# Order of the input products and the latent queries' path in the first block of a two-part network on Trainium2

## Chip, cores and metric

The kernel runs on one core of one Trainium2 chip. The metric is the device time of one execution in microseconds; of the kernel before, three runs gave a median of 1709.43 us (1709.2 to 1711.75).

## What is computed

Two networks of depth 2 follow each other on 256 latent tokens (width 1024). The first also carries 256 context tokens. The change is in the first, whose block is, cut to what matters:

```
def first_block(...):
    for i in range(DEPTH):                      # 2
        hc = modulate(rms_norm(x_ctx, g_norm1[i]), csh1, csc1)
        h = modulate(rms_norm(x_lat, g_norm1[i]), sh1, sc1)
        # h @ w_in -> q (6 heads x 64), k, v (2 x 64), cq (256), ckv (128), k_rope (32), pool input (256)
        # qm = rms_norm(cq) @ w_uq : 6 latent queries x 96;  km, vm = rms_norm(ckv) @ w_ukv
        # q, k normed per head and rotated; of qm and km the last 32 columns are rotated
        mix = concat([attention(q, k, v), attention(qm, km, vm),
                      multiscale_pool(pool_in, w_pool, ls_pool)]) @ w_out
        x_lat = x_lat + gt1 * mix
        x_lat = x_lat + gt2 * sq_relu_mlp(modulate(rms_norm(x_lat, g_norm2[i]), sh2, sc2))
        # block 0 does the same for the context tokens; block 1 only takes keys and values from them
```

Context tokens attend to context keys alone, latent tokens to both. The second network (two layers with differential attention and an mLSTM) isn't touched.

## The kernel before

Every engine has its own program, written out by hand, and they meet in semaphores; no scheduler moves anything. Weights come from memory through a ring of three slots of 2048 KB that SP fills (L991); a slot's transfer starts when the slot three before it has been used. Large products are made of three fp32r products: ScalarE rounds a granule of a weight (two chunks of 128 rows) to its high part (`hi_to`, L1892), VectorE makes the low part (`lo_to`, L2509), and TensorE's `in_granule(n, m)` (L1444 to L1446) multiplies granule m of input slot n for up to four tiles of 128 tokens: high by high, high by low and low by high. The granules of a block's input slots are w0 to w0+11, four in each slot.

Below, PE is TensorE, ACT is ScalarE, DVE is VectorE and POOL is GpSimd. `w_in` has three input slots in a block. Slot A holds keys, values, the latent keys' source and the shared rope key (416 columns); slot C the latent queries' source cq and the pool's input (512; 256 in block 1, where p0 and p1 are multiplied apart, L1412, from weights that `shift_products`, L2569 and L2572 on DVE, scales); slot B the attention's queries (384). The order is A, C, B. Block 0 multiplies four token tiles, block 1 for C and B two.

Between and behind these products lies what this text calls the units: transposes (`turned_over`, L1456), latent keys and values (L1472), latent queries qm (L1489), and on the way to each the norms and rotations. ACT takes products out of PSUM (L2011, L2028, L2034, L2042, L2046; Tk, Tkm, Tqm, Tq are the transposed keys, latent keys, latent queries and queries) and takes roots (L1953 to L1955). DVE sums squares (L2580), refines the roots (L2586, L2587), multiplies by cosines (L2655, L2666, L2673) and scales (L2648, L2682). POOL makes the halves swapped and multiplied by sines (L1067), adds them (L1079, L1107, L1115), scales the rope keys (L1094) and makes the pool's window sums (L1137 to L1156). The last things before the attention are 24 (block 1: 12) transposes Tqm and 12 (6) transposes Tq.

The attention runs in steps j, one 128-row tile of queries for a pair of heads in each. Block 0 has 24 steps (two sets of tokens), block 1 has 12. In step j PE makes the scores of j (L1568), transposes the weights of j-2 (L1586) and every second step multiplies by the values (L1600); DVE takes the maximum (L2746) and scales by the reciprocal sum (L2756, L2757), ACT takes the exponential (L2103) and copies transposed weights (L2093). The pairs of latent heads begin at step 12 in block 0 and at step 6 in block 1. In block 0 some steps also hold products for the modulation (`mod_products`, L1320; `mod_column`, L1330; their sums on DVE L2450 and L2451).

At the start, `shift_hi` (ACT, L1912) and `modulated_norm` (DVE, L2549 and L2521) make the eight chunks of the normed, modulated tokens as a high and a low part, while ACT and DVE split the first weights between them:

```
if not which and k in (1, 4, 6):
    lo_to(first_gran["win", i] + {1: 1, 4: 2, 6: 3}[k])
```

## Time and profile before

| | us |
|---|---|
| median of three runs (lowest, highest) | 1709.43 (1709.2, 1711.75) |
| the profiled execution's own time | 1707.64 |
| its span in the trace | 1705.9 |
| PE busy | 1638.3 (96%) |
| DVE, ACT, POOL busy | 1149.5, 907.6, 487.8 |
| attention of block 0, of block 1 begins at | 134.62, 702.95 |

The span is what lies between the first and last instruction of the profiled execution, 1.7 us short of that execution's time. In the page, busy time is a share of the span; "PEclk" is the granted clock of PE as a share of full speed, its mean 0.988 here. A row of the timeline has start and duration in us, engine, line, operation, what it writes and reads, the count of merged instructions, and in brackets the idle time before it and what ended that.

### The profile page before, as it was taken

What the parts mean: (1) busy time and instruction counts of PE and PEld (TensorE: products, weight loads), DVE (VectorE), ACT (ScalarE), POOL (GpSimd) and SP (SyncE); (2) the same over time, 40 slices, a digit from 0 to 9 for tenths busy, and PEclk for the clock granted to TensorE, in tenths of its full rate; (3) what the DMA queues carried; (4) which work ended last, traced back from release to release, by engine and by line L of the source; (5) the groups of instructions that cost most, each with busy time, mean ns of one, the idle gap of its engine ahead of it and who ended that gap; (6) DMA issues with size and microseconds to landing.
All of it is one profiled execution on the core that took longest, in us unless ns stands there. A gap on an engine that the chain in (4) does not pass through costs nothing.

```text
span 1705.9 us, 27966 instructions
## 1 busy us (share of the span) xinstructions
PE 1638.3 (96%) x10354; PEld 1405.9 (82%) x10354; DVE 1149.5 (67%) x2027; ACT 907.6 (53%) x1970; POOL 487.8 (29%) x936
## 2 busy tenths in 40 slices
PE   5998998999999998898999999999999999999998
PEld 3874586888888878577999887899899878999998
DVE  5567847878787347876555678785556787775555
ACT  4455625444353535656555666675544665764542
POOL 2442014000000021502000124177752161586720
PEclk9998999999999999999999999999999999999999
DMA  9524225554445322114455445333255445333450
GB/s 364 178 87 161 100 73 179 197 192 169 182 176 177 132 87 99 50 50 149 164 184 195 152 162 191 137 137 129 100 198 175 173 148 177 134 134 115 149 198 26
DMA packets 106377, 254.95 MB, mean 149 GB/s; under 512 B 2742, under 2 KB 9540, under 8 KB 103172
## 3 DMA queue, kind: packets, MB, share of 16 engines
q1 hardware_dynamic: 104874, 250.57, 41.2%
q0 software_dynamic: 1088, 2.56, 0.7%
q8 instruction: 84, 1.38, 0.3%
q14 instruction: 49, 0.40, 0.1%
q10 hardware_dynamic: 282, 0.04, 0.0%
HBM read 252.11 MB, written 1.05 MB: 148 GB/s over the span
## 4 chain that ended last, share of the span: by engine, by line
PE 84%; DVE 8%; ACT 4%; DMA 2%; issue 1%; POOL 1%; SPq 0%; DVEq 0%; ACTq 0%; POOLq 0%
PE ps L1361 19%; PE ps L1363 18%; PE ps L1362 18%; PE ps L1568 2%; PE ps L1664 2%; PE ps L1665 2%; PE ps L1666 2%; DVE big_r L2509 2%; PE ps L1600 2%; PE ps L1444 2%; PE ps L1445 2%; PE ps L1586 2%; PE ps L1446 2%; ACT big_r L1892 1%; PE ps L1783 1%
## 5 line engine op out<-in xcount | busy, mean ns | idle before, releaser
L1892 ACT ACTIVATE big_r<-ring 128x1024 fp32r<-128x1024 f32 (+2 forms) x224 | 235.3, 1051 | 377.1 <-PE ps L1363 352.3
L2509 DVE TENSOR_TENSOR big_r<-ring,big_r 128x1024 fp32r<-128x1024 f32 (+2 forms) x224 | 275.5, 1230 | 230.8 <-ACT big_r L1892 230.4
L1362 PE MATMUL ps<-big_r 128*128 128x256 f32 (+1 forms) x1064 | 352.9, 332 | 0.0
L1361 PE MATMUL ps<-hT_r,big_r 128*128 128x256 f32 (+1 forms) x768 | 245.7, 320 | 0.4 <-DVE big_r L2509 0.4
L1361 PE MATMUL ps<-big_r 128*128 128x256 f32 (+1 forms) x720 | 240.4, 334 | 3.6 <-DVE big_r L2509 1.7
L1363 PE MATMUL ps<-hT_r,big_r 128*128 128x256 f32 (+1 forms) x768 | 242.1, 315 | 0.0
L1363 PE MATMUL ps<-big_r 128*128 128x256 f32 (+1 forms) x720 | 237.9, 330 | 0.0
L1025 POOL TENSOR_TENSOR sq<-sq 128x256 f32<-128x256 f32 (+1 forms) x30 | 35.5, 1185 | 705.6 <-ACT sq L1852 704.1
L1362 PEld LDWEIGHTS ps<-big_r 128*128 128x128 f32 x1064 | 202.2, 190 | 18.4
L1361 PEld LDWEIGHTS ps<-hT_r,big_r 128*128 128x128 f32 x768 | 146.3, 190 | 9.6 <-issue 1.0
L1363 PEld LDWEIGHTS ps<-hT_r,big_r 128*128 128x128 f32 x768 | 146.2, 190 | 9.4
L1361 PEld LDWEIGHTS ps<-big_r 128*128 128x128 f32 x720 | 136.7, 190 | 18.6 <-issue 3.3
L1363 PEld LDWEIGHTS ps<-big_r 128*128 128x128 f32 x720 | 136.7, 190 | 12.8
L2509 DVE TENSOR_TENSOR cst_r<-ring,w_ukv_sb_r 128x1024 fp32r<-128x1024 f32 x70 | 88.5, 1264 | 54.1 <-ACT w_ukv_sb_r L1892 54.1
L1892 ACT ACTIVATE w_ukv_sb_r<-ring 128x1024 fp32r<-128x1024 f32 x70 | 74.1, 1059 | 85.3 <-PE ps L1363 73.2
L2475 DVE SCALAR_TENSOR_TENSOR pT<-ring,csilu,pT 128x512 f32<-128x512 f32 x168 | 118.5, 748 | 1.3
L1892 ACT ACTIVATE nt_r<-ring 128x1024 fp32r<-128x1024 f32 (+2 forms) x54 | 55.9, 1036 | 77.7 <-PE ps L1363 73.1
L2509 DVE TENSOR_TENSOR rstd_r<-ring,nt_r 128x1024 fp32r<-128x1024 f32 (+2 forms) x54 | 64.9, 1202 | 45.3 <-ACT nt_r L1892 45.1
L1361 PE MATMUL ps<-hT_r,w_ukv_sb_r 128*128 128x256 f32 x304 | 88.3, 290 | 0.0
L1363 PE MATMUL ps<-hT_r,cst_r 128*128 128x256 f32 x304 | 85.9, 283 | 0.0
L1362 PE MATMUL ps<-xT_r,nt_r 128*128 128x256 f32 x304 | 85.7, 282 | 0.0
L1362 PE MATMUL ps<-xT_r,w_ukv_sb_r 128*128 128x256 f32 x296 | 83.6, 282 | 0.0
(432 smaller groups left out, 4273.2 us busy)
## 6 DMA issues: line engine op xcount, KB each, us to landing
ring<-in_w_in SPq DMA_DIRECT2D x42, 2048.0 KB, 7.8
ring<-in_w_mlp SPq DMA_DIRECT2D x32, 2048.0 KB, 8.7
ring<-in_w_mod SPq DMA_DIRECT2D x24, 2048.0 KB, 7.8
ring<-in_w_out SPq DMA_DIRECT2D x4, 2048.0 KB, 7.9
ring<-in_w_out_a SPq DMA_DIRECT2D x4, 2048.0 KB, 7.9
ring<-in_w_out_b SPq DMA_DIRECT2D x4, 2048.0 KB, 7.9
ring<-in_w_o SPq DMA_DIRECT2D x4, 2048.0 KB, 8.1
ring<-in_w_in SPq DMA_DIRECT2D x2, 1664.0 KB, 9.0
```

The costliest lines, as they stand in the source:

```text
L1025: nc.gpsimd.tensor_tensor(sum_slot(0, T), sum_slot(0, T), sum_slot(k, T), ALU.add).then_inc(sq_summed, 1)
L1361: mm(b[:, 0:T], w_hi[:, k, :], hi(k), start=(j == 0), stop=False)
L1362: mm(b[:, 0:T], w_hi[:, k, :], lo(k), start=False, stop=False)
L1363: last = mm(b[:, 0:T], w_lo[:, k, :], hi(k), start=False, stop=(j == KC - 1))
L1444: mm(b, x_hi, w_hi[:, k, :], start=(m == 0 and k == 0), stop=False)
L1445: mm(b, x_hi, w_lo[:, k, :], start=False, stop=False)
L1446: last = mm(b, x_lo, w_hi[:, k, :], start=False, stop=(m == 3 and k == 1))
L1568: fill(mm(banks[e][:, 0:tiles * P], lhs, rhs, start=True, stop=True), (tag, "s", 2 * j + e))
L1586: last = tr(b[:, t * P:(t + 1) * P], weights(u)[:, t * P:(t + 1) * P], IDENT)
L1892: act_fn(hi, raw, ACT.Copy).then_inc(hi_ready, 1)
L2475: ins = V.scalar_tensor_tensor(acc, w, c, acc, ALU.mult, ALU.add)
L2509: V.tensor_tensor(lo, raw, hi.bitcast(F32), ALU.subtract).then_inc(lo_ready, 1)
```

## The change

It has these parts.

1. The first input slot of block 0 comes in two transfers of half the rows. ACT rounds its first granule when the first half has landed, and the second granule at k = 1 of `shift_hi` rather than ahead of it; DVE makes the second low part at k = 2 rather than 1. PE awaits the tokens' high parts chunk by chunk, and multiplies slot A chunk by chunk over the tiles.
2. The slots' order is A, B, C; the host puts the weight's columns in that order. Block 1's `shift_products` and p0, p1 now read the third slot.
3. Units of block 0: B's granules with the latent values between them, then C's with Tk and Tq between them, Tkm, the modulation's unit 4, Tcq, Tp, unit 5, and the qm products as the last thing before the attention. Units of block 1: C m0 to m2, Tk, C m3, Tkm, Tcq, the qm products, Tq.
4. Latent queries are multiplied by cosines, scaled (in three pairs of heads) and transposed (to bank 7) between the attention's steps: DVE in `latent_queries_made`, PE at the end of a step in `TURN_STEPS`, ACT with a copy behind the exponentials of the same step. At a latent pair's first step PE awaits the copies of its two heads.
5. POOL's window sums: in block 1 ahead of all units, in block 0 behind the queries. ACT's copies of block 1's queries await them. Several buffers move; three of the four modulation products in the attention go to later steps.

```diff
-MOD_STEPS = {1: 6, 7: 7, 13: 8, 19: 9}
+MOD_STEPS = {1: 6, 8: 7, 16: 8, 20: 9}
+TURN_STEPS = ({6: 0, 7: 1, 12: 2, 13: 3, 14: 4, 15: 5}, {4: 0, 5: 1, 6: 2, 7: 3, 8: 4, 9: 5})
+SCALE_STEPS = ({5: 0, 10: 1, 11: 2}, {3: 0, 4: 1, 6: 2})
-WIN_NAMES = "ACB"
+WIN_NAMES = "ABC"
...
+                if key == ("win", 0, 0):
+                    k0 = KC // 2
+                    sp.dma_start(ring[:, r, 0:k0, 0:src.shape[2]], src[:, 0:k0, :]).then_inc(head_landed, 16)
+                sp.dma_start(ring[:, r, k0:KC, 0:src.shape[2]], src[:, k0:KC, :]).then_inc(slot_landed[r], 16)
...
-                    if n == 0:
-                        pe.wait_ge(h_ready, h_before + 2 * m + 2)
+                    by_chunk = [(t, k) for k in range(2) for t in keys]
+                    for t, k in by_chunk if n == 0 else [(t, k) for t in keys for k in range(2)]:
+                        if n == 0 and t == 0:
+                            pe.wait_ge(h_ready, h_before + 2 * m + k + 1)
...
+                        if pair[0] >= GQ and s == 0 and j % 2 == 0:
+                            for h in pair:
+                                await_drained(pe, (tag, "Tqm", h - GQ))
...
+                    if j in TURN_STEPS[i]:
+                        h = TURN_STEPS[i][j]
+                        pe.wait_ge(qm_scaled, 3 * i + h // 2 + 1)
+                        turned_over(("Tqm", h), [qm_raw[t][:, h, :] for t in tiles_q])
...
+                    if j == 0:
+                        lo = tiles_of(i)[0]
+                        small_root(5 * i + 5, qm_ms[:, lo:], qm_r[:, lo:], qm_r2[:, lo:], MQK)
+                    if j in TURN_STEPS[i]:
+                        h = TURN_STEPS[i][j]
+                        key = (tag, "Tqm", h)
+                        await_bank(act, key)
+                        drain(act_fn(qmT[0:MQK, h, t0:TOK], bank(key)[0:MQK, 0:TOK - t0], ACT.Copy), key)
...
-                n = slot_no["win", 1, 1]
+                n = slot_no["win", 1, 2]
                 dve.wait_ge(slot_landed[n % RING], landed_at[n])
...
+                    for c in range(2):
+                        pool_summed(i, c)
+                units(i)
...
+            def latent_queries_made(i, j):
+                if j == 1:
+                    refined(5 * i + 5, qm_ms[:, lo:], qm_r[:, lo:], qm_r2[:, lo:], MQK)
...
+                if j < n_q:
+                    t = lo + j
...
+                    V.tensor_tensor(qm_raw[t], qm_raw[t], qm_cos[:, t].unsqueeze(1).to_broadcast([P, MH, MQK]), ALU.mult)\
+                        .then_inc(qm_cosined, 1)
+                if j in SCALE_STEPS[i]:
+                    p = SCALE_STEPS[i][j]
...
+                    x = qm_all[:, lo:, 2 * p:2 * p + 2, :]
+                    V.tensor_tensor(x, x, qm_c[:, lo:, 2 * p:2 * p + 2].unsqueeze(3).to_broadcast([P, n_q, 2, MQK]), ALU.mult)\
+                        .then_inc(qm_scaled, 1)
```

Three places show what this moves. First POOL at the entry of block 1's units, before (L1067 turns the keys' halves; the window sums stand 20 instructions on):

```order
L1129 MEMSET big 128x1088 [waits bank7_filled]
L1067 TENSOR_TENSOR turns_72<-big,cst 128x4x32 [waits raw_copied,unit_tables_made]
L1067 TENSOR_TENSOR turns_72<-big,cst 128x4x32
L1067 TENSOR_TENSOR turns_72<-big,cst 128x2x16 [waits kr_copied]
L1067 TENSOR_TENSOR turns_72<-big,cst 128x2x16
L1079 TENSOR_TENSOR big<-big,turns_72 128x256 [waits k_cosined,k_swapped]
```

and the entry of the keys' turning after the change (here L1143 to L1157 are the window sums, L1086 the halves, L1098 the add; two shifts, L1177, and six sums stand ahead of these rows):

```order
L1144 TENSOR_TENSOR big<-big 128x269 [waits pool_chain]
L1146 TENSOR_TENSOR big<-big 128x265 [waits pool_chain]
L1147 TENSOR_TENSOR big<-big 128x256 [waits pool_chain]
L1152 TENSOR_TENSOR big<-big,cst 64x256 [waits pool_chain]
L1152 TENSOR_TENSOR big<-big,cst 64x256
L1157 TENSOR_TENSOR big<-big 128x256 [waits pool_chain]
L1086 TENSOR_TENSOR turns_72<-big,cst 128x4x32 [waits raw_copied,unit_tables_made]
L1086 TENSOR_TENSOR turns_72<-big,cst 128x4x32
L1086 TENSOR_TENSOR turns_72<-big,cst 128x2x16 [waits kr_copied]
L1086 TENSOR_TENSOR turns_72<-big,cst 128x2x16
L1098 TENSOR_TENSOR big<-big,turns_72 128x256 [waits k_cosined,k_swapped]
```

The fourteen instructions of the shift and the window sums now stand ahead of the keys' turning. Second, DVE in block 1's units after the change, from the refined latent keys' roots (L2709) on; L2579 makes low parts (w0+10 and w0+11 here), L2714 multiplies queries by cosines, L2722 and L2727 scale queries and latent keys:

```order
L2709 TENSOR_TENSOR big<-big 128x24 [waits dve_chain]
L2579 TENSOR_TENSOR rstd_r<-ring,nt_r 128x2x256 [waits hi_ready]
L2714 TENSOR_TENSOR big<-big,cst 128x384 [waits q_swapped] x2
L2656 SCALAR_TENSOR_TENSOR big<-big 128x12 [waits roots_made]
L2657 SCALAR_TENSOR_TENSOR big<-big 128x12 [waits dve_chain]
L2579 TENSOR_TENSOR big_r<-ring,big_r 128x2x256 [waits hi_ready,dve_chain]
L2722 TENSOR_TENSOR big<-big 128x384 [waits q_added,q_cosined] x2
L2727 TENSOR_TENSOR big<-big 128x6x64 [waits km_rooted]
```

The low part of C's last granule comes behind two products that await POOL's `q_swapped`; before, it came right behind the latent keys' roots. Third, PE around the first latent step of block 1's attention (j = 6), before:

```order
L1586 MATMUL ps<-cst,sq 128x128 [waits p_ready,bank5_drained]
L1586 MATMUL ps<-cst,sq 128x128 x3
L1568 MATMUL ps<-big 128x512 [waits bank3_drained,bank2_drained,bank1_drained,bank0_drained]
L1568 MATMUL ps<-big 128x512
L1586 MATMUL ps<-cst,pb 128x128 [waits p_ready,bank4_drained]
```

and after, where L1489 is the transpose Tqm, L1614 the scores and L1632 the weights' transposes:

```order
L1632 MATMUL ps<-cst,sq 128x128 [waits p_ready,bank5_drained]
L1632 MATMUL ps<-cst,sq 128x128 x3
L1489 MATMUL ps<-cst,hT 96x128 [waits bank7_drained,qm_scaled]
L1489 MATMUL ps<-cst,hT 96x128
L1614 MATMUL ps<-big 128x512 [waits bank1_drained,bank3_drained,bank2_drained,bank7_drained,bank0_drained]
L1614 MATMUL ps<-big 128x512
L1632 MATMUL ps<-cst,pb 128x128 [waits p_ready,bank4_drained]
```

The scores now await bank 7, which the transposes just ahead of them fill and ACT drains.

## Rows read from the trace of the kernel before

**Rows 1.** Part 1 of the page, PE's busy time.
```profile
PE 1638.3 (96%) x10354; PEld 1405.9 (82%) x10354; DVE 1149.5 (67%) x2027; ACT 907.6 (53%) x1970; POOL 487.8 (29%) x936
```
**Rows 2.** Stretches: length; PE, PEld, DVE, ACT, POOL busy; granted clock; DMA share; GB/s.
```profile
130.00:140.00 10.00, 8.31 (x36) 4.97 (x36) 3.11 (x11) 3.85 (x11) 9.53 (x12) 0.52 0.42 175
134.60:182.00 47.40, 46.44 (x283) 23.67 (x284) 37.98 (x112) 28.59 (x88) 5.51 (x7) 0.95 0.34 117
700.00:710.00 10.00, 7.18 (x23) 3.12 (x24) 4.94 (x10) 4.31 (x12) 9.12 (x13) 0.69 0.00 0
```
**Rows 3.** Timeline of DVE at the start.
```profile
34.54 1.02 DVE L2509 TENSOR_TENSOR pT_r<-ring,pT_r 128x832 fp32r<-128x832 f32 x1 [3.43 <-ACT pT_r L1892]
```
**Rows 4.** Timeline of PE at the start: modulation column, then the first product of A.
```profile
37.31 1.11 PE L1330 MATMUL ps<-cst,big 128*128 128x128 f32 x4 [4.36 <-DVE mod L2451]
41.00 0.71 PE L1444 MATMUL ps<-pT_r,hT_r 128*128 128x416 f32 x1 [2.57 <-DVE big_r L2521]
```
**Rows 5.** Timeline of PE at the end of block 0's units.
```profile
119.53 1.13 PE L1456 MATMUL ps<-cst,big 128*96 128x128 f32 x8 [2.45 <-ACT big L2034]
130.70 2.92 PE L1456 MATMUL ps<-cst,hT 128*128 128x128 f32 x12 [3.42 <-DVE hT L2682]
134.62 1.22 PE L1568 MATMUL ps<-big 64*128 64x256 f32 x4 [0.99 <-ACT big L2046]
```
**Rows 6.** The stretch with block 0's transposes Tqm, PE alone: busy, then clock.
```profile
124.10:127.30 3.20, 3.14 (x28) 1.00 0.80 338
```
**Rows 7.** Timeline of DVE at the end of block 0's units.
```profile
116.33 0.75 DVE L2666 TENSOR_TENSOR big<-big 128x576 f32<-128x576 f32 x1
126.62 4.02 DVE L2682 TENSOR_TENSOR hT<-hT,big 128x384 f32<-128x384 f32 x4
```
**Rows 8.** SP's queue: issues of block 1's second and third input slots.
```profile
604.25 22.13 SPq L991 DMA_DIRECT2D ring<-in_w_in  x2
```
**Rows 9.** Part 6 of the page: transfers of the input slots, KB, us to landing.
```profile
ring<-in_w_in SPq DMA_DIRECT2D x42, 2048.0 KB, 7.8
```
**Rows 10.** Timeline of DVE around block 1's entry, then in its units.
```profile
629.81 0.34 DVE L2569 TENSOR_SCALAR big<-ring,mod 128x256 f32<-128x256 f32 x1
634.46 0.88 DVE L2691 SCALAR_TENSOR_TENSOR xT<-ps,mod,xT 128x256 f32<-128x256 f32 x2 [1.68 <-PE ps L1363]
...
683.32 0.18 DVE L2643 TENSOR_TENSOR big<-big 128x24 f32<-128x24 f32 x1
685.60 3.09 DVE L2648 TENSOR_TENSOR big<-big 128x384 f32<-128x384 f32 x4
```
**Rows 11.** Timeline of POOL in block 1's units.
```profile
664.87 0.88 POOL L1067 TENSOR_TENSOR turns<-big,cst 128x128 f32<-128x128 f32 x2 [29.38 <-ACT big L1971]
...
683.58 4.03 POOL L1094 TENSOR_TENSOR big<-big 128x192 f32<-128x192 f32 x4 [5.03 <-DVE big L2643]
...
693.40 3.46 POOL L1067 TENSOR_TENSOR hT<-hT,cst 128x192 f32<-128x192 f32 x4 [1.06 <-ACT sq L1948]
```
**Rows 12.** The stretch with block 1's shift and window sums, POOL alone.
```profile
699.30:711.20 11.90, 10.94 (x15) 0.71 0.00 0
```
**Rows 13.** Timeline of PE in block 1: units, then the attention.
```profile
672.10 5.33 PE L1472 MATMUL ps<-w_ukv_sb,big 128*128 128x384 f32 x16
...
683.74 4.04 PE L1489 MATMUL ps<-w_uq_sb,big 128*128 128x288 f32 x16
...
702.95 3.56 PE L1568 MATMUL ps<-big 64*128 64x512 f32 x8 [0.78 <-ACT big L2046]
...
719.14 1.88 PE L1568 MATMUL ps<-big 96*128 96x512 f32 x4
```
**Rows 14.** Timeline of ACT: six copies Tqm; the end of step 5's exponentials.
```profile
697.66 1.72 ACT L2042 ACTIVATE big<-ps 96x256 f32<-96x256 f32 x6
...
721.11 0.22 ACT L2103 ACTIVATION_READ_ACCUMULATOR sq<-ps,stat 128x1 f32 x1
```

More of the change, by code:

```diff
@@ L234, in plan_banks @@
             take((tag, "o", g), 6)
[L235 to L238 removed]
+        for j in range(2 * len(groups_of(i))):
+            if i == 0 and j in MOD_STEPS:
+                take((tag, "modrow", MOD_STEPS[j]), 7)
+                take((tag, "modcol", MOD_STEPS[j]), 7)
+            if j in TURN_STEPS[i]:
+                take((tag, "Tqm", TURN_STEPS[i][j]), 7)
         for c in range(2):
```

393 lines of the change are left out of this document (210 added, 183 removed).

## The prediction

> **What bounds the kernel now.** I read the page first. PE is busy for 1638.3 us, 96% of the span [rows 1]; DVE has two thirds of it, ACT half. So a wait moved off PE is worth its own length, and one put on PE costs it. Next come the stretches around the change: where do PE and DVE stand close together, and where is the granted clock low? In the ten us from 130 on the clock is 0.52 with PE busy for 8.31, and around block 1's entry to the attention it is 0.69 [rows 2]; both come behind short idle times of PE. Then the timelines: at the start PE waits 4.36 us for a modulation column and 2.57 for the first tokens [rows 4]; at the end of block 0's units it waits 2.45, 3.42 and 0.99 us [rows 5]. In block 0's attention to 182 us PE is busy for 46.44 of 47.40 us, DVE for 37.98 [rows 2]: PE leads, and DVE has 9.4 us free.
>
> 0.2% of this kernel is 3.4 us, about what a measurement can tell from no change. The sum is made against the profiled execution, whose 1707.64 us stand 1.8 under the median of three; the difference is then put on the median.
>
> **The start.** DVE's queue stands 3.43 us for ACT's first rounding, which awaits the whole first slot [rows 3]; the copy and sums that release PE's 4.36 us wait are behind it [rows 4]. With half a slot the rounding comes earlier, and chunk-wise waiting takes about one round of DVE (0.9 us) from the second wait. I take 4.0 us at A's first product (41.00) and 4.5 at its end, since part of its first matmuls ran slow behind that idle time. Bounds: 2.5, if DVE then feeds PE chunk by chunk too slowly, and 6.9, both waits.
>
> **Block 0's units.** Order B, C puts the query norms and the rotations of DVE and POOL beside C's products. The wait of 3.42 us stands behind four scalings that took 4.02 us [rows 5, 7], and this work now ends well ahead; so go 2.45 + 3.42 + 0.99 = 6.9 us [rows 5]. The 12 transposes Tq took 2.92 us right behind an idle time, where eight took 1.13 [rows 5]; at that rate they take 1.4 to 1.7, so 1.4 us go. The 24 transposes Tqm are in a stretch of 3.2 us [rows 6]; 3.1 leave the units. What is late next is the qm products' way out of PSUM, needed only by DVE in the steps. With the start, 4.5 + 6.9 + 1.4 + 3.1 = 15.9 us at the attention's first scores. The clock of 0.52 [rows 2] also lay over the attention's first five us, where about half of some 4.5 busy us, 2.2 us, is gained: 18.1.
>
> **What the steps of block 0 give back.** DVE gets, ahead of the first output's copy, four sums and four cosine products of 576 columns. A product took 0.75 us with POOL quiet [rows 7]; scalings of 384 columns beside POOL took 4.02 / 4 = 1.0 each [rows 7], and by their widths 576 columns come to 1.5. POOL now makes window sums just then; I take 1.0 each, 4.0 together, and 1.6 for what of the sums comes later than the first scores: 5.6. Three scalings of 768 columns (about 1 us each, by 0.75 for 576) and the root's refinement, 3.5 together, then use up DVE's free time save some 1.9 us of delay. On PE, Tqm of heads 0 and 1 fall where DVE leads; four heads, 4 x 3.1 / 6 = 2.1, are paid (1.8 without the gaps), and bank 7, now shared with the modulation's products, costs about 0.5. In all 5.6 + 1.9 + 1.8 + 0.5 = 9.8; block 0 gains 18.1 - 9.8 = 8.3 us. Bounds: 12, if DVE's free 9.4 us swallow most of it, and 5, if every addition to DVE (4 x 1.5 + 1.6 + 3.5 = 11.1) is on PE's path.
>
> The Trainium skill's page "GPSIMD Engine Reference", section 1 (Specifications), says that GpSimd shares its SBUF interfaces with VectorE and contends with its instructions of two SBUF inputs. The four scalings fit that, while POOL was busy for most of their time; by that rule all four cosine products would take 1.5 us, and block 0 would gain 2 us less.
>
> **Block 1's entry.** The second and third input slots are issued at about 604.3 and 626 [rows 8]. Before, `shift_products` read the second, long landed at 629.81 [rows 10]. Now it reads the third, which holds 2048 KB; such a transfer takes 7.8 us from issue to landing [rows 9], so this one lands at about 634. DVE stands for some 4 us ahead of the residual's add at 634.46 [rows 10], three products of 0.9 us come between, and the add is 1.5 to 2.5 us late. Behind it are PE's p0 and p1. I take 1.6; bounds 0, if DVE catches up, and 2.5.
>
> **Block 1's units.** POOL's shift and window sums fill a stretch of 11.9 us [rows 12]. Before they lay behind the queries, beside the attention, and cost nobody anything. Now they begin when p0 and p1 are copied, near 659, and end near 671; the keys' turning that began at 664.87 [rows 11] begins 6.6 us later. DVE's cosine of the keys waits for it, and behind it in DVE's queue stands the low part of B's last granule: PE reaches the latent values near 677.4 instead of 672.10 [rows 13]. The latent keys' roots follow at about 685.9 instead of 683.32 [rows 10] (some other work lay between before). Then POOL: rope keys 4.03, halves of the queries 3.46 [rows 11], until 693.4; DVE's cosines wait for them, and behind the cosines is the low part of C's last granule. So PE, done with C m2 and Tk near 688, stands until about 694.2. From there follow C m3 (1.4), scalings 1.7 and latent keys 3.09 on DVE [rows 10] with PE waiting, 24 transposes Tkm (3.1, by rows 6), Tcq 0.5, the qm products 4.04 [rows 13], Tq and its copies 2.0, and about 0.5 at slow clock: the first scores at 709.0 instead of 702.95 [rows 13], 6.1 us later, though 12 transposes have left. Bounds: 3, if rotation and POOL overlap better, and 9, if the clock falls as in [rows 2] over C m3 to qm.
>
> **Block 1's steps.** Here PE leads. The 12 transposes cost 1.3 us. The latent pairs need two heads each, and the second head's Tqm is transposed at the end of the step before its first use. ACT's queue has that copy behind the step's exponentials: those of step 5 end at 721.11 + 0.22 = 721.33 [rows 14], a copy takes 1.72 / 6 = 0.29 [rows 14], so scores can start at 721.6, where they would at 719.14 + 0.2 [rows 13]: 2.3 us. Steps 8 and 10 repeat the pattern, so it comes three times: 6.9. ACT has no work that could make up for it, since its exponentials follow PE's scores. Bounds: 4, if the pause lets DVE and ACT get ahead for the next, and 10, with the clock lowered.
>
> **The sum.** Block 1: 6.1 (with the entry's 1.6 inside) + 1.3 + 6.9 = 14.3 us lost. Block 0: 8.3 gained. The rest, from block 1's output product on, is unchanged. Together +6 us: 1709.4 + 6 = 1715 us.
>
> **Rivals.**
> (a) *Block 1 keeps its time* (the other side). If exponentials of step 5 don't hold back the copies, or DVE's low part does not really end behind POOL's halves, block 1 loses only the entry's 1.6 and the transposes' 1.3, 3 to 6 us, against 8 to 12 in block 0: 1700 to 1706, likeliest 1704. It decides where the keys' turning on POOL still ends before DVE comes to it. Against it: POOL's order and the rows of POOL. For it: my times for block 1 are chained over ten steps, each of which can be a little shorter. Chance 0.22.
> (b) *The two sides cancel*, with DVE's free time in block 0 taking the additions (12 gained) and block 1 losing 10 to 14: within 3.4 us of 1709.4. Chance 0.25.
> (c) *The clock falls in block 1*, at C m3 and behind each pause in the steps: 4 to 6 us more, 1719 to 1723. For it are 0.52 and 0.69 [rows 2] behind pauses of 1 to 3.4 us [rows 5]. Chance 0.15. The Trainium skill's page "TensorE: Matmul & The Clock Gate", section "Why this matters for your kernels", asks that PE not stand idle between bursts and speaks for this rival; by it the sum would be about 1720.
> (d) The forecast, 1713 to 1719: chance 0.38.
>
> **How the numbers follow.** Slower by over 0.2% is (c) and (d): 0.53. Within it is (b), 0.25, and faster by more (a), 0.22. The likeliest case's own range is 1711 to 1719. The range reaches well into (a) below and to the end of (c) above: 1701 to 1723.
>
> **What would show it.** The profile of the changed kernel should have A's first product near 37, no PE wait over 1 us ahead of block 0's attention, which begins near 118.5, and that attention some 8 us longer to its end. In block 1 PE should stand for about 6 us for DVE's low part at C m3, the first scores should come about 6 us later relative to the end of block 0, and there should be waits of 2.3 us for ACT's copy of Tqm at steps 6, 8 and 10. I am wrong if those waits are short, if POOL's window sums end before ACT's roots of the keys are needed, or if block 0's attention does not grow.

## Result, and the profile after the change

The changed kernel takes 1740.86 us (median of four runs, 1738.95 to 1741.6) against 1709.71 for the kernel before, run beside it: a ratio of 1.0178 with a 95% interval of 1.0161 to 1.0196, so 31 us slower. I had forecast 1715, and a range that ended at 1723. The page of the kernel after, its first lines:

```profile
span 1739.7 us, 27978 instructions
PE 1655.0 (95%) x10354; PEld 1417.1 (81%) x10354; DVE 1151.0 (66%) x2027; ACT 906.6 (52%) x1970; POOL 485.7 (28%) x936
```

The span grew by 33.8 us. PE has the same 10354 instructions as in [rows 1] and is busy for 16.7 us more with them; the other 17.1 us are idle time. So half of the loss is PE standing still and half is PE working slowly. Where, the timeline of PE in the kernel after shows (start, duration, engine, line, operation, count, idle time before it and what ended that):

```profile
37.09 0.46 PE L1477 MATMUL ps<-pT_r,hT_r 128*128 128x416 f32 x1 [2.25 <-DVE pT_r L2579]
...
120.75 0.70 PE L1614 MATMUL ps<-big 64*128 64x256 f32 x4
...
130.79 1.39 PE L1632 MATMUL ps<-cst,pb 128*128 128x128 f32 x4 [3.59 <-DVE pb L2841]
...
152.91 1.06 PE L1353 MATMUL ps<-ring,cwide 128*32 128x512 f32 x8 [1.33 <-ACT big L2174]
...
262.65 1.12 PE L1326 MATMUL ps<-sq,cst 128*128 128x512 f32 x2 [0.96 <-ACT sq L1902]
...
639.33 2.08 PE L1326 MATMUL ps<-sq,cst 128*128 128x512 f32 x2 [3.47 <-ACT sq L1902]
641.20 9.09 PE L1445 MATMUL ps<-big,ring 128*128 128x256 f32 x32
...
701.19 0.58 PE L1477 MATMUL ps<-big_r,hT_r 128*128 128x256 f32 x1 [5.21 <-DVE big_r L2579]
...
717.60 1.99 PE L1614 MATMUL ps<-big 64*128 64x512 f32 x8 [1.33 <-ACT big L2053]
...
739.44 2.37 PE L1614 MATMUL ps<-big 96*128 96x512 f32 x4 [2.42 <-ACT big L2174]
...
751.16 3.75 PE L1614 MATMUL ps<-big 96*128 96x512 f32 x4 [2.22 <-ACT big L2174]
...
808.06 0.67 PE L1324 MATMUL ps<-sq,cst 128*128 128x256 f32 x2 [2.59 <-POOL sq L1044]
```

For the same landmarks, three more rows of the timeline of PE in the kernel before: the second norm of block 0, the first of block 1 and the second of block 1.

```profile
261.95 1.12 PE L1293 MATMUL ps<-sq,cst 128*128 128x512 f32 x2 [0.75 <-ACT sq L1852]
...
636.10 1.12 PE L1293 MATMUL ps<-sq,cst 128*128 128x512 f32 x2 [0.82 <-ACT sq L1852]
...
775.43 0.67 PE L1291 MATMUL ps<-sq,cst 128*128 128x256 f32 x2 [2.60 <-POOL sq L1025]
```

Read against these and [rows 4, 5, 13]: A's first product comes 3.9 us earlier, the first scores of block 0 13.9 us earlier, but block 0's second norm 0.7 later. From there to block 1's first norm 2.5 us are lost, from that norm to block 1's first scores 11.4 (78.3 instead of 66.9 us), from those to the second norm 18.0 (90.5 instead of 72.5), and 1.2 in all the rest. That is 33.8. Every wait that the prediction looked for is there, the 2.2 to 2.4 us at the latent steps of block 1 too (the row at 751.16 has a twin at 764.54); but block 0's attention, up to its second norm, is 14.6 us longer and not 8. Stretches of the kernel after, all engines, in the columns of [rows 2]:

```profile
120.00:130.00 10.00, 6.38 (x40) 2.40 (x38) 8.50 (x18) 4.00 (x15) 8.41 (x11) 0.99 0.26 75
130.00:140.00 10.00, 8.36 (x28) 4.46 (x28) 9.79 (x23) 4.91 (x13) 3.81 (x6) 0.50 0.40 165
...
740.00:750.00 10.00, 8.94 (x44) 5.23 (x42) 6.31 (x15) 4.53 (x11) 0.00 (x0) 0.83 0.00 0
750.00:760.00 10.00, 8.84 (x32) 4.91 (x33) 3.28 (x8) 3.98 (x12) 0.00 (x0) 0.66 0.01 2
760.00:770.00 10.00, 7.78 (x35) 4.19 (x35) 5.04 (x13) 5.20 (x12) 0.00 (x0) 0.83 0.00 1
```

A granted clock of 0.66 over ten us means that PE ran at the lower of its two levels, 1.2 GHz, for two thirds of them. The row at 751.16 is such a piece: four scores take 3.75 us where they took 1.88 in [rows 13].

### The profile page after: what moved, and what is told of

Same layout as the page of the kernel before. It is cut to its first block, busy times and chain, and to the rows that moved or that the text cites. A ratio compares the mean times of both kernels' runs of the same rounds, so it can differ in the third digit from the quotient of the medians.

```text
span 1739.7 us, 27978 instructions
## 1 busy us (share of the span) xinstructions
PE 1655.0 (95%) x10354; PEld 1417.1 (81%) x10354; DVE 1151.0 (66%) x2027; ACT 906.6 (52%) x1970; POOL 485.7 (28%) x936
## 3 DMA queue, kind: packets, MB, share of 16 engines
HBM read 252.11 MB, written 1.05 MB: 146 GB/s over the span
## 4 chain that ended last, share of the span: by engine, by line
PE 50%; DVE 6%; ACT 3%; POOL 1%; issue 1%; DVEq 0%; ACTq 0%; POOLq 0%
PE ps L1394 11%; PE ps L1396 11%; PE ps L1395 11%; PE ps L1714 2%; PE ps L1715 2%; PE ps L1716 2%; DVE big_r L2579 2%; PE ps L1614 1%; PE ps L1833 1%; PE ps L1836 1%; PE ps L1828 1%; ACT big_r L1945 1%; PE ps L1632 1%; PE ps L1646 1%; DVE cst_r L2579 1%
## 5 line engine op out<-in xcount | busy, mean ns | idle before, releaser
L2579 DVE TENSOR_TENSOR big_r<-ring,big_r 128x1024 fp32r<-128x1024 f32 (+2 forms) x224 | 277.1, 1237 | 229.5 <-ACT big_r L1945 228.9
L2579 DVE TENSOR_TENSOR cst_r<-ring,w_ukv_sb_r 128x1024 fp32r<-128x1024 f32 x70 | 88.3, 1262 | 54.6 <-ACT w_ukv_sb_r L1945 54.6
L2579 DVE TENSOR_TENSOR rstd_r<-ring,nt_r 128x1024 fp32r<-128x1024 f32 (+2 forms) x54 | 66.0, 1223 | 47.2 <-ACT nt_r L1945 47.1
L1395 PE MATMUL ps<-xT_r,big_r 128*128 128x256 f32 x296 | 83.6, 283 | 0.0
```

Of the source, the lines that this page charges most:

```text
L1395: mm(b[:, 0:T], w_hi[:, k, :], lo(k), start=False, stop=False)
L2579: V.tensor_tensor(lo, raw, hi.bitcast(F32), ALU.subtract).then_inc(lo_ready, 1)
```

## Experiments

### Block 1's transposes one step earlier

```diff
-TURN_STEPS = ({6: 0, 7: 1, 12: 2, 13: 3, 14: 4, 15: 5}, {4: 0, 5: 1, 6: 2, 7: 3, 8: 4, 9: 5})
-SCALE_STEPS = ({5: 0, 10: 1, 11: 2}, {3: 0, 4: 1, 6: 2})
+TURN_STEPS = ({6: 0, 7: 1, 12: 2, 13: 3, 14: 4, 15: 5}, {3: 0, 4: 1, 5: 2, 6: 3, 7: 4, 8: 5})
+SCALE_STEPS = ({5: 0, 10: 1, 11: 2}, {2: 0, 3: 1, 5: 2})
```

> The change, with block 1's latent queries scaled and transposed one step earlier (head h's transposes at the end of step 3 + h), so that ACT's copy of a pair's second head stands behind the exponentials of a step before the one ahead of its use. Nothing else moves. Theory A (the three waits of 2.2 to 2.4 us at steps 6, 8 and 10 are the cause and each pulls the granted clock down behind it): the waits go, 6.9 us, and the stretches at 0.66 to 0.83 return to 1.0, some 5 to 7 us more; 1727 to 1729 us instead of 1740.9. Theory B (the clock stays low in block 1's attention because of the idle times at its entry, whatever the steps do): only the waits go, about 1734. Theory C (the wait is elsewhere by then): above 1738.

1723.08 us (ratio to the kernel before 1.0079, 1.0064 to 1.0094), 17.8 under the change. First scores and second norm of block 1 in its timeline of PE, and one stretch of the attention between them, all engines:

```profile
715.35 1.99 PE L1614 MATMUL ps<-big 64*128 64x512 f32 x8 [1.33 <-ACT big L2053]
...
791.53 0.67 PE L1324 MATMUL ps<-sq,cst 128*128 128x256 f32 x2 [2.59 <-POOL sq L1044]
```
```profile
737.60:747.60 10.00, 10.00 (x63) 5.97 (x62) 7.71 (x21) 7.66 (x21) 0.00 (x0) 1.00 0.01 2
```

No wait for ACT's copy is left in the steps, and in this stretch the clock is at 1.00 and PE is busy throughout. From first scores to second norm it takes 76.2 us instead of 90.5. These are the two stretches, PE alone (length, busy, clock, DMA share, GB/s), of the kernel after and then of the experiment:

```profile
717.60:808.06 90.46, 75.86 (x448) 0.89 0.12 42
```
```profile
715.35:791.53 76.18, 68.44 (x448) 0.96 0.14 50
```

So 14.3 us hung on the copy's place. PE's idle time is shorter by 6.9 us, the three waits, and the same 448 instructions are busy for 7.4 us less, the slow clock behind them. Theory A holds, and even it priced the clock too low: in these two executions a wait of 2.3 us cost 4.8. (The other 3.5 of the 17.8 us don't belong to the edit: the first scores themselves are 2.3 us earlier, 1.3 of them already ahead of block 1's norm, and the norm's two matmuls ran at full clock behind the same wait in this execution.) The clock's share is not the same in every execution; the last section shows the same three waits without it.

### Block 1's window sums behind the units

```diff
-                    for c in range(2):
-                        u = upad[:, c, 1, PAD:PAD + SEQ]
-                        link(nc.gpsimd.tensor_scalar(u, u, small[:, 24 + c:25 + c], None, ALU.add))
-                    for c in range(2):
-                        pool_summed(i, c)
                 units(i)
...
                 latent_queries_added(i)
+                if i:
+                    await_bank(pool, (tag, "Tkm", MH - 1))
+                    for c in range(2):
+                        u = upad[:, c, 1, PAD:PAD + SEQ]
+                        link(nc.gpsimd.tensor_scalar(u, u, small[:, 24 + c:25 + c], None, ALU.add))
+                    for c in range(2):
+                        pool_summed(i, c)
...
-                if i:
-                    act.wait_ge(pooled, 6)
```

> The change, with block 1's shift and window sums on POOL moved behind everything else of its units and the latent queries (their buffer is then the one block 0 uses, which is free when the latent keys are transposed), and without ACT's wait for them ahead of its copies of the queries. Theory A (the sums ahead of the keys' turning hold back DVE's low parts, and with these PE, all through block 1's units): the turning begins near 663 instead of 675.3, the low part of the fourth query granule is no longer behind it, the latent values start 4 us or more earlier; 1740.9 - 5 to 8 = 1733 to 1736. Theory B (what comes late is the chain latent values, roots, rope keys, halves, low part, whatever the sums do): under 3 us, about 1739.

1729.70 us (1.0115, 1.0100 to 1.0131), 11.2 under the change, more than either theory gave. The timeline of POOL in the kernel after shows where its sums lay and that the keys' turning came behind them:

```profile
662.32 2.72 POOL L1177 TENSOR_SCALAR big<-big,small 128x256 f32<-128x256 f32 x2 [26.25 <-DVE big L2818]
...
675.33 1.79 POOL L1086 TENSOR_TENSOR turns<-big,cst 128x128 f32<-128x128 f32 x4
```

In the timeline of PE of the experiment the wait for the fourth query granule is gone, first scores are 5.6 us earlier (1.4 of that by an earlier norm of block 1 and by full clock at it, 4.2 in the units), and the attention behind them is 3.9 shorter although its steps are the same:

```profile
712.04 3.48 PE L1616 MATMUL ps<-big 64*128 64x512 f32 x8 [1.33 <-ACT big L2055]
...
798.63 0.67 PE L1326 MATMUL ps<-sq,cst 128*128 128x256 f32 x2 [2.59 <-POOL sq L1044]
```

### Both of these together

> The change with both edits of block 1 together: latent queries one step earlier, and POOL's sums behind the units. Theory A (two separate losses, one in the attention's steps and one in the units ahead of them): they add, 17.8 + 11.2 = 29.0 us under 1740.9, so 1711.9, within 1.5. Theory B (part of the 11.2 us of the second edit came from a clock that stood better in steps that the first edit repairs anyway): 3 us or more less than the sum, 1715 or above.

1721.34 us (1.0063, 1.0043 to 1.0083), with runs from 1717.06 to 1724.96. Not 29.0 us but 19.5 are gained: Theory B's number. Its first scores are at 711.10, 4.3 earlier than with the first edit alone, and from there to the second norm it takes 75.8 us, as with the first edit. The 3.9 us by which the second edit alone had shortened the attention are not there again. They were clock: the same three waits are in that trace, but PE is busy for 72.4 us there instead of 75.9. That an earlier start brought the better clock is not shown; a version below ("Block 0 without DVE's added work") has the same steps at full clock without this edit. The second edit is worth 4.3 us at the first scores by these two traces, and 1.7 by the medians (1723.08 and 1721.34). The four runs with both edits lie 7.9 us apart, so its size is not settled better than that.

### The shift's products behind the last residual

```diff
-                        if i == 0 and key[2] == BLOCKS - 1 and key[3] >= KC - 2:
-                            shift_products(*((0, 4) if key[3] == KC - 2 else (4, KC)))
+                        if i == 0 and key[2] == BLOCKS - 1 and key[3] == KC - 1:
+                            shift_products(0, KC)
```

> As both1, and DVE makes all eight products of the shift with block 1's third slot behind the last residual instead of four of them ahead of it. Theory A (the wait for the third slot's DMA, landed at 635.4, stands ahead of the last add and PE's norm, and PE's 3.5 us of idle time there pull the clock down over p0, p1): PE's idle time at the norm falls from 3.5 to about 1 us; 3 to 4 us under both1. Theory B (the products then come too late for PE's shifted columns and for the norm's reciprocal on DVE): 0 to 1 us.

1717.26 us (1.0039, 1.0024 to 1.0054), 4.1 under both edits: Theory A. (The intervals of the two overlap a little; the first scores come 4.5 us earlier, at 706.62.) The wait that it takes away, in the timeline of DVE of the kernel after, is for a transfer:

```profile
635.45 0.76 DVE L2639 TENSOR_SCALAR big<-ring,mod 128x256 f32<-128x256 f32 x1 [4.98 <-DMA ring<-in_w_in]
```

and the norm on PE in the experiment waits for 0.82 us instead of 3.47:

```profile
635.49 1.13 PE L1328 MATMUL ps<-sq,cst 128*128 128x512 f32 x2 [0.82 <-ACT sq L1904]
```

### C's last low part ahead of the queries' cosines

```diff
                 lo_to(w0 + 11)
-                for t in tiles_q:
-                    if t >= 2:
-                        dve.wait_ge(q_swapped, 4 * i + 2 * t - 2)
-                    V.tensor_tensor(q_raw[t], q_raw[t], q_cos[:, t].unsqueeze(1).to_broadcast([P, GQ, HD]), ALU.mult)\
-                        .then_inc(q_cosined, 1)
-                refined(5 * i + 3, q_ms[:, lo:], q_r[:, lo:], q_r2[:, lo:], HD)
                 lo_to(w0 + 12)
...
                 refined(5 * i + 4, cq_ms[:, lo:], cq_r[:, lo:], cq_r2[:, lo:], QR)
                 link(V.tensor_tensor(cq_t[:, lo:], cq_r[:, lo:], cq_r[:, lo:], ALU.mult))
+                if i:
+                    for t in tiles_q:
+                        if t >= 2:
+                            dve.wait_ge(q_swapped, 4 * i + 2 * t - 2)
+                        V.tensor_tensor(q_raw[t], q_raw[t], q_cos[:, t].unsqueeze(1).to_broadcast([P, GQ, HD]), ALU.mult)\
+                            .then_inc(q_cosined, 1)
+                    refined(5 * i + 3, q_ms[:, lo:], q_r[:, lo:], q_r2[:, lo:], HD)
```

The queries' scaling follows there too, and for block 0 all of it stays where it was.

> As both1, and in block 1 DVE makes the low part of C's last granule right behind the one before it, then scales the latent keys and takes cq out of PSUM, and only then multiplies and scales the queries, which PE turns over last. Theory A (the low part behind POOL's halves of the queries is what PE awaits at C's last granule, 4.7 us even without the sums): that wait is under 1 us, of which some comes back as a wait for the scaled latent keys; 3 to 5 us under both1. Theory B (the latent keys' roots and rope keys come no earlier, and the wait only moves to the transposes Tkm): under 1.5 us.

1716.30 us (1.0037, 1.0025 to 1.0049), 5.0 under both edits: Theory A. First scores come at 705.44 instead of 711.10, and the wait at C's last granule, 4.67 us with both edits, is gone; about 1 us of the 5.7 is again the norm at full clock. In the timeline of DVE of the kernel after the stall is plain: the latent keys' roots are ready at 693.02, then DVE stands for POOL.

```profile
693.02 0.18 DVE L2709 TENSOR_TENSOR big<-big 128x24 f32<-128x24 f32 x1
693.12 0.68 DVE L2579 TENSOR_TENSOR rstd_r<-ring,nt_r 128x512 fp32r<-128x512 f32 x1
696.70 0.93 DVE L2714 TENSOR_TENSOR big<-big,cst 128x384 f32<-128x384 f32 x1 [2.90 <-POOL st_c L1086]
```

### Block 0: cosines two steps later

The first scaling goes from step 5 to step 6 with them.

```diff
-                if j == 1:
+                jc = j if i else j - 2
+                if jc == 1:
...
-                if j < n_q:
-                    t = lo + j
+                if 0 <= jc < n_q:
+                    t = lo + jc
```

> The change, with block 0's four cosine products and the refinement of the roots two steps later (j = 2 to 5 instead of 0 to 3), and the first scaling at step 6 instead of 5. Theory A (DVE's additions in the first two steps, when PE has nothing yet to do but wait for the first weights, leave PE idle for 3.6 us at 130.8 and bring the clock of 0.50 that follows to 141): the idle time falls under 2 us, the clock stays, 5 to 7 us are gained: about 1735. Theory B (DVE has so much to do in steps 0 to 11 that it sets their pace wherever the products stand): under 2 us, about 1740.

1736.95 us (1.0157, 1.0140 to 1.0174), 3.9 under the change, between the theories. Its timeline of PE says that little of this is block 0's: the wait of 3.59 us is now several, 4.35 us together, and block 0's second norm comes at 261.85, 0.8 earlier than with the change. The clock stood at 0.88 from 130 to 140 instead of 0.50, and hardly any time came of it, as PE then waited for DVE instead. That is Theory B's mechanism.

```profile
129.79 0.41 PE L1632 MATMUL ps<-cst,pb 128*128 128x128 f32 x2 [1.06 <-DVE pb L2842]
...
133.21 0.41 PE L1632 MATMUL ps<-cst,pb 128*128 128x128 f32 x2 [1.21 <-DVE pb L2842]
...
137.65 1.71 PE L1632 MATMUL ps<-cst,pb 128*128 128x128 f32 x7 [2.08 <-DVE pb L2842]
```

### Block 0: transposes one step earlier, bank 7 free

```diff
-TURN_STEPS = ({6: 0, 7: 1, 12: 2, 13: 3, 14: 4, 15: 5}, ...
-SCALE_STEPS = ({5: 0, 10: 1, 11: 2}, ...
+TURN_STEPS = ({5: 0, 6: 1, 11: 2, 12: 3, 13: 4, 14: 5}, ...
+SCALE_STEPS = ({4: 0, 10: 1, 11: 2}, ...
```

> As both1, and block 0's transposes of the latent queries one step earlier each (5, 6, 11, 12, 13, 14; first scaling at step 4), so that no product for the modulation stands right behind one in the bank they share. Theory A (PE's waits of 1.3 and 1.1 us ahead of the modulation's products at 152.9 and 180.7 are for ACT's copies out of bank 7): both go, 2.4 us under both1. Theory B (PE waits for DVE there anyway, in step with its maxima and scalings): under 1 us.

1720.04 us (1.0052, 1.0035 to 1.0069), 1.3 under both edits and within their spread. The waits of 1.33 and 1.10 us for ACT are gone, and block 0's second norm is at 262.81, where it was 262.31 with both edits alone. Theory B: PE meets DVE there in any case. In place of both, and of a wait of 1.39 us for DVE at 166.42, its timeline of PE has one for DVE's sum of the modulation:

```profile
165.53 1.06 PE L1491 MATMUL ps<-cst,hT 128*96 128x128 f32 x4 [3.14 <-DVE mod L2521]
```

### The cosines on POOL, and POOL kept quiet

Here POOL multiplies by the cosines, ahead of its adds, and block 0's second window sum comes behind them:

```diff
-                    V.tensor_tensor(qm_raw[t], qm_raw[t], qm_cos[:, t]..., ALU.mult).then_inc(qm_cosined, 1)
+                for t in tiles_of(i):
+                    nc.gpsimd.tensor_tensor(qm_raw[t], qm_raw[t], qm_cos[:, t]..., ALU.mult).then_inc(qm_cosined, 1)
```

> The change, with the cosine products of the latent queries (four in block 0, two in block 1) on POOL instead of between DVE's maxima and scalings, ahead of POOL's adds, and block 0's second window sum behind them. Theory A (DVE's own work sets the pace of block 0's steps 0 to 11, which shifting the products by two steps could not change): PE's idle time of 3.6 us at 130.8 falls under 1 us, the clock stays above 0.9 there, block 0's attention ends 5 to 8 us earlier, and block 1's first weights' transposes wait under 1.5 us instead of 2.15: 1740.9 - 7 = about 1734. Theory B (DVE and POOL get into each other's way, so that the products cost DVE as much from there, or the scaling at step 5 comes late): under 2 us.

1734.72 us (1.0133, 1.0102 to 1.0164), its runs from 1728.86 to 1739.69; PE's idle time at block 0's entry is 4.26 us, not under 1. The median is Theory A's, the trace is Theory B's: its block 0 takes as long as the change's, although DVE lost its products. The four runs are two pairs, 1728.86 and 1729.85 at a mean granted clock of 0.988, 1739.59 (the profiled one) and 1739.69 at 0.980, so the 6 us of the median are not shown to be this edit's. The next run moved only the window sum:

```diff
-                if i == 0:
-                    await_drained(pool, (tag, "Tp", 1))
-                    pool_summed(i, 1)
                 latent_queries_added(i)
+                if i == 0:
+                    await_drained(pool, (tag, "Tp", 1))
+                    pool_summed(i, 1)
```

> The change, with POOL's second window sum of block 0 moved behind its adds to the latent queries, so that POOL does nothing while DVE refines the roots of the latent queries and multiplies by the cosines in steps 0 to 2; DVE's work is that of the change. Theory A (DVE's products and its tiny two-input operations, 24 columns in 1.1 to 1.3 us, wait for POOL's instructions; that is what stretches DVE's queue ahead of the first weights): these take 0.17 to 0.2 us, the cosines 0.75, PE's idle time at 130.8 falls from 3.6 to under 2 us and the clock of 0.50 that follows rises; 3 to 6 us under 1740.9. Theory B (the count of DVE's instructions is what counts, POOL's company costs under 1 us): above 1739.

1738.04 us (1.0156, 1.0140 to 1.0172), 2.8 under the change, with block 0's second norm at 261.20, 1.5 earlier. DVE's operations are as short as Theory A had them and PE's first wait is under 2 us; the clock does not rise, and the gain is just under its range. Even that is near what the traces scatter by: six of them (the change and five versions that edit only block 1 or its entry) have the same steps in block 0, and from the first scores to the second norm they take 140.1 to 141.9 us. Here it is 140.1. The same operations in the timeline of DVE, of the kernel after and then of this one:

```profile
124.12 1.15 DVE L2757 TENSOR_TENSOR hT<-hT,cst 128x576 f32<-128x576 f32 x1
...
126.50 1.14 DVE L2751 TENSOR_TENSOR big<-big 128x24 f32<-128x24 f32 x1
```
```profile
123.58 0.75 DVE L2757 TENSOR_TENSOR hT<-hT,cst 128x576 f32<-128x576 f32 x1
...
125.57 0.18 DVE L2751 TENSOR_TENSOR big<-big 128x24 f32<-128x24 f32 x1
```

PE's first wait fell to 1.58 us, and yet the clock fell as before; a wait of 1.20 follows:

```profile
128.25 0.87 PE L1632 MATMUL ps<-cst,pb 128*128 128x128 f32 x4 [1.58 <-DVE pb L2841]
...
131.45 0.66 PE L1632 MATMUL ps<-cst,pb 128*128 128x128 f32 x2 [1.20 <-DVE pb L2841]
```
```profile
130.00:140.00 10.00, 8.05 (x32) 4.47 (x32) 9.75 (x21) 5.20 (x16) 5.99 (x6) 0.50 0.34 143
```

### Block 0 without DVE's added work

These two leave out the cosines and the scaling of block 0's latent queries; empty instructions keep the order.

```diff
+                    if i == 0:
+                        dve.nop().then_inc(qm_cosined, 1)
...
+                    if i == 0:
+                        dve.nop().then_inc(qm_scaled, 1)
```

> The change without DVE's four cosine products and three scalings of block 0's latent queries (empty instructions release what waited for them; the latent queries of block 0 are then not rotated fully and not scaled). DVE does 3.8 + 2.9 us less in steps 0 to 11; the refined roots and POOL's window sum stay. Theory A (DVE's additions are what eats the 14 us that the attention of block 0 starts earlier): block 0's second norm on PE, at 262.65 with the change, comes 7 us or more earlier. Theory B (the tiny operations that wait for POOL at the entry, bank 7's waits and the low clock behind the entry's idle time are enough): 3 us or less.

1732.13 us (1.0141, 1.0124 to 1.0158). In the timeline of PE block 0's second norm comes 5.8 us earlier than with the change (6.7 if measured from the first scores, 121.6 here):

```profile
256.81 1.12 PE L1326 MATMUL ps<-sq,cst 128*128 128x512 f32 x2 [0.77 <-ACT sq L1902]
```

From the first scores to that norm, PE alone, in the kernel before, the kernel after and this version:

```profile
134.62:261.95 127.33, 124.34 (x678) 0.98 0.28 100
```
```profile
120.75:262.65 141.90, 130.48 (x702) 0.95 0.26 90
```
```profile
121.60:256.81 135.21, 126.74 (x703) 0.99 0.27 94
```

> The same with POOL's second window sum behind its adds, so that neither DVE's work nor POOL's company is left at the entry. Theory A of the run before: 1 to 2 us more than it. Theory B: PE's idle time at the entry falls under 1.5 us and 3 us or more come on top of that run.

1733.82 us (1.0133, 1.0104 to 1.0162), runs from 1723.99 to 1735.84, second norm at 256.53: nothing on top. So DVE's added work is worth 6.7 us in block 0 against the change, 3.0 of it idle time of PE and 3.7 busy time, and at least 4.9 against the quickest trace with block 0's steps unchanged (140.1 us); POOL's company is worth little once that work is gone. Some 8 us of the 14.6 that the steps cost are left without it, and so is most of PE's wait at the entry: 2.58 us instead of 3.59. Of the expectations the first is nearer to Theory A, short of its 7 us; of the second neither fits, as PE's waits at the entry are 1.05 and 1.31 us and the gain was under 1 us.

### Part 1 of the change alone, on the kernel before

```diff
+                if key == ("win", 0, 0):
+                    k0 = KC // 2
+                    sp.dma_start(ring[:, r, 0:k0, 0:src.shape[2]], src[:, 0:k0, :]).then_inc(head_landed, 16)
...
+                        if k == 1:
+                            hi_to(w0 + 1)
-                    if not which and k in (1, 4, 6):
+                    if not which and k in (2, 4, 6):
...
+                            pe.wait_ge(h_ready, h_before + 2 * m + k + 1)
```

> The kernel before, with part 1 of the change alone: the first slot in two transfers, the second granule rounded at k = 1, the low part at k = 2, PE waiting chunk by chunk. Theory A (what the start gained, 3.9 us at A's first product, reaches the end): 1709.5 - 4 = 1705.5. Theory B (the earlier start is lost again in a wait further on, for a slot or for POOL's tables of block 0): 1708 to 1710.

1705.61 us over ten runs (1704.88 to 1707.41); ratio 0.9977, interval 0.9968 to 0.9986. By its number this is Theory A: 4.1 us faster, the fastest version found. The trace doesn't show these 4 us arriving in one piece. Counted from the first modulation column (27.33 here, 25.69 before) A's first product is 4.0 us earlier and block 0's first scores, behind a wait of 3.68 us where it was 3.42, only 2.5. Of the rest some is clock: from block 0's second norm to block 1's first it takes 1.9 us less, though the instructions are the same. So the part's worth is measured; that all of it is the earlier first product is not shown.

### Everything repaired

> All edits that gained: block 1's latent queries one step earlier, its window sums behind the units, the third slot's shift products behind the last residual, the low part of C's last granule ahead of the queries' cosines, and the cosine products on POOL. Theory A (the losses are separate, save the overlap of the first two): 1721.3 - 4.1 - 5.0 - 6 = 1706, which is faster than the kernel before by 4 us. Theory B (what is left at the two entries to the attention, where PE has only scores to make until DVE has scaled the first weights, brings the clock down whatever is repaired elsewhere): 1710 to 1713, no faster than before.

1708.24 us over eleven runs; 0.9988, interval 0.9979 to 0.9997, 1.5 us under the kernel before and 32.6 under the change. That lies between the theories: faster than before, if barely, which Theory B excluded, and 2.2 us above Theory A. Without its first part, if that is worth 4.1 here too (not run), the repaired change would be slower than the kernel before. With the cosines back on DVE and POOL quiet:

> The repaired version with the cosines back on DVE and POOL's second window sum of block 0 behind its adds (block 1's latent queries one step earlier, its window sums behind the units, shift products behind the last residual, C's last low part ahead of the queries' cosines). Theory A (contention with POOL was the price at block 0's entry): 2 to 4 us under the 1708.2 of the version with the cosines on POOL, so 1704 to 1706. Theory B: 1708 or more, as the cosines are on DVE again.

1710.42 us over eleven runs; 1.0004, interval 0.9995 to 1.0013: Theory B. The two differ by 2.2 us the other way than Theory A had it; block 0 takes 141.9 us in this trace and 139.6 in the repaired one, so there the cosines on POOL did gain something behind the entry.

## Why the prediction was wrong, point by point

**The start** was right: 4.0 us forecast, 3.9 measured at A's first product, and 4.1 at the end of the program when made alone; that the two agree so closely is in part luck (see the experiment).

**Block 0's units** were near: 15.9 us forecast, 13.9 came. A wait of 1.08 us at 80.56, for ACT to empty B's banks ahead of C, is one piece of the rest; the kernel before had none there.

**What the steps of block 0 give back** failed. They took 14.6 us more (8.4 idle, 6.1 busy), where I had 9.8 less the 2.2 of a regained clock, 7.6. DVE's additions cost 6.7 by the experiment (4.9 at least), against 7.5 in my sum (5.6 + 1.9), so that term's size stands. What is left without them, 7.9 us, I had put at 0.1 (1.8 + 0.5 - 2.2), and all three of these terms were mis-sized. The clock's 2.2 us were not regained: it is 0.50 from 130 to 140 again, now behind DVE's 3.59 us. The transposes are paid in full, 24 of them, about 3.1 us at the rate of [rows 6] and not 1.8. And PE's idle time, for which I had only the 0.5 of bank 7, is 5.5 us longer than before even without DVE's additions. Part of it is three waits ahead of the modulation's products, 1.33 and 1.10 us for ACT's copies out of bank 7 and 0.53 for DVE's sum; moving the transposes away from that bank gained nothing, as PE then waited for DVE. The other part is the start of the attention, which I did not price: in steps 0 and 1 PE has nothing but scores until DVE has scaled the first weights, so it stands for DVE there, 2.58 us even without the cosines. The rows showed DVE with 9.4 us free over 47 [rows 2]; little of that was free in the first twenty (8.50 and 9.79 busy of 10). Block 0's gain of 8.3 was a loss of 0.7.

**Block 1's entry**: forecast 1.6, bounds 0 to 2.5. The norm came 2.5 late, and behind PE's 3.47 us the p0 and p1 products took 9.09 us instead of about 7; A's products started 4.6 late. The experiment gave 4.1 back. The mechanism was named; DVE's first product behind the transfer began at 635.45 where I had the landing at 634, and the clock, which I had left out, took its share of p0 and p1. The upper bound was too low by both.

**Block 1's units**: 4.5 beyond the entry forecast, bounds 1.4 to 7.4, 10.1 measured from A's first product on. The places were right (the wait at C's last granule was 5.21 us; I had 6.2), but the chain ahead of it was too short: I let the latent keys' roots come at 685.9, 2.6 us later than before, and they came at 693.0. I had shifted PE's latent values by 5.3 us and then the roots behind them by only half of that, though everything between them waits in turn. The values themselves came 10.4 us later (682.50), 4.6 of them already lost at A's first product: POOL's sums began at 662.32, not near 659, and its turning of the keys at 675.33, not near 671.5. My sum had a slip too: the terms listed from 694.2 on come to 16.3 us, so 710.5 and not 709.0, unless some overlap, which I did not say. The two orders, POOL's and DVE's, were worth 4.3 us at the first scores (1.7 by the medians) and 5.0.

**Block 1's steps**: the three waits were forecast at 2.3 us each and are 2.42, 2.22 and 2.22. What failed is the sentence that they cost 6.9: 14.3 us came back with them. The 7.4 us on top are the clock, which I had put into rival (c) with 4 to 6 us for all of block 1 and a chance of 0.15. I had in hand that pauses of 1 to 3.4 us had brought 0.52 and 0.69 [rows 2, 5], and treated this as a risk, where it came in full in five of the seven traces with these three waits. The Trainium skill's page "TensorE: Matmul & The Clock Gate", section "Why this matters for your kernels", asks that PE not stand idle between bursts, but it warns of longer gaps than these. The trace goes further than the page: behind waits of 2.2 to 2.4 us the rows above have 0.83, 0.66 and 0.83. Another 3.7 us of the steps are left after the experiment, against 1.3 forecast for the transposes: at the attention's first steps PE waits 1.46 and 2.15 us where it waited 0.84 and 0.60 before.

Forecast and profiled execution (6 and 33.8 us over that of before) are 27.8 us apart: 9.0 in block 0, 7.8 on the way from there to block 1's first scores (13.9 against 6.1), 9.8 in block 1's steps (18.0 against 8.2), and 1.2 in the rest.

## What to carry over

In a kernel where PE is busy for 96%, price every new wait of PE at its length and once more for the clock behind it, as the upper end of a range whose lower end is the length alone; sum the busy time too, since the same instructions took 16.7 us more. When a step is put between others, check for each engine's queue where its result stands behind something it doesn't need: one step earlier for a copy was worth 14.3 us in the attention, and an engine's mean free time says nothing of the first steps, in which the pipeline is still filling. Try the parts of a change one by one: one that gained 4.1 us was buried under 35.

## What was not expected of the hardware

**The same wait does not always bring the clock down.** PE's 3.47 us ahead of block 1's first norm is in eleven traces, the same to the hundredth. In five of them (the change among them) the two matmuls behind it took 2.07 or 2.08 us, in the other six 1.12 or 1.13. Two of these, from the timelines of PE of both edits together and of the first edit alone:

```profile
638.09 2.07 PE L1328 MATMUL ps<-sq,cst 128*128 128x512 f32 x2 [3.47 <-ACT sq L1904]
```
```profile
638.04 1.12 PE L1326 MATMUL ps<-sq,cst 128*128 128x512 f32 x2 [3.47 <-ACT sq L1902]
```

The three waits in block 1's steps show it at a larger scale. Seven traces have all three, each the same within 0.1 us. In five of them the attention takes 90.0 to 91.8 us from its first scores to the second norm; in one (window sums behind the units) 86.6; in the first version without DVE's work in block 0, whose block 1 is that of the change, 83.0, with the clock at 1.00 in each ten us from 730 to 770. Its second wait, in the timeline of PE, where the change's scores took 3.75 us:

```profile
743.15 1.96 PE L1614 MATMUL ps<-big 96*128 96x512 f32 x4 [2.22 <-ACT big L2174]
```

Against the 76.2 us without the waits, they cost 6.8 us there, their bare length, and 14.3 in the change. What decides between the two is open.

The spread from run to run goes with the clock as well. The four runs of the last version without DVE's work are 1723.99 us at a mean granted clock of 0.989 and 1732.99 to 1735.84 at 0.982 to 0.983; those with the cosines on POOL are the two pairs above, 10.8 us apart; the ten runs of the first part alone stay within 2.5 us, at 0.986 to 0.988. Many waits don't make a spread by themselves: the change itself has them all, and its four runs lie within 2.7 us, at 0.979 to 0.982.

**A tiny operation can cost as much as POOL's whole instruction.** Beside POOL, DVE's product of 24 columns took 1.14 us, and in the repaired version 1.32; alone it took 0.18. In the kernel after it ended with POOL's instruction, at 127.64 and 127.60 (a profile has POOL's times only roughly); another of 24 columns that began at 125.86, shortly before POOL's one ended at 126.21, took 0.38. The timeline of DVE of the repaired version, then POOL's at that time:

```profile
126.92 1.33 DVE L2660 SCALAR_TENSOR_TENSOR big<-big 128x24 f32<-128x24 f32 x1
128.29 1.32 DVE L2769 TENSOR_TENSOR big<-big 128x24 f32<-128x24 f32 x1
```
```profile
124.08 5.49 POOL L1134 TENSOR_TENSOR hT<-hT,cst 128x576 f32<-128x576 f32 x4
```

Each lasted about as long as one of POOL's four products (5.49 / 4 = 1.37 us). The Trainium skill's page "GPSIMD Engine Reference", section 1 (Specifications), names this contention for DVE's instructions with two SBUF inputs; the trace agrees and gives the price, which doesn't go by the instruction's own size. So work moved from DVE to POOL slows what stays on DVE, and moving the cosines bought nothing at block 0's entry (PE's wait there was 4.26 us instead of 3.59).
